# The seam between two transformer-like blocks: token sums as ones-matrix products, a 512-wide norm factor, and another order of the work around it

## What is computed

```
x = rms_norm(x + merged @ w_out, final_g)              # end of the first block
h = concatenate([meta, x])
hn = rms_norm(h, norm1_g)                              # start of the second
f_in, qkv, z, ab, gate_f, gate_d = split(hn @ w_in)
g = -exp(a_log) * softplus(a + dt_bias)                # a, b: 32 columns of ab
beta = sigmoid(b)
qkv = silu(conv5(qkv)); q, k = l2_normalize(q), l2_normalize(k)
... fourier mixing of f_in, gated delta rule forward and backward over q, k, v, g, beta ...
h = h + mixer(h); h = h + mixture_of_experts(h)        # 64 experts, fp32 weights
out = rms_norm(h, final_norm_g)[:, 16:]
```

## Time and profile before

| | |
|---|---|
| median of 3 runs | 1282.62 us (1280.85 to 1285.04) |
| the profiled execution | 1281.57 us, span 1279.6 us |
| instructions | 20485 |
| busy share PE / PEld / DVE / ACT / POOL | 87 / 70 / 37 / 29 / 30 % |
| chain that ended last | PE 59 %, DMA 24 %, DVE 10 %, issue 3 %, ACT 2 % |

### The profile page before, as it was taken

One profiled execution on the slowest core, in us unless ns is written; L12 is line 12 of the kernel. 1 busy time (PEld: TensorE's weight loads), 2 busy tenths in 40 slices (PEclk: granted clock), 3 DMA queues, 4 the chain that ended last, 5 costly groups with the idle time before them and its releaser, 6 DMA issues.

```text
span 1279.6 us, 20485 instructions
## 1 busy us (share of the span) xinstructions
PE 1118.5 (87%) x8376; PEld 893.3 (70%) x8376; DVE 475.8 (37%) x941; ACT 368.5 (29%) x553; POOL 380.7 (30%) x175
## 2 busy tenths in 40 slices
PE   9998999999999799979999999897777776666776
PEld 7987899999999787979888978653333343333334
DVE  3333842911123365543886342321112222211113
ACT  4533334443446364442435200310000000000001
POOL 4834849788776253443103000000000000000000
PEclk8998899999998699989999999998888888888898
DMA  6632636465656233331322037999999999999994
GB/s 227 197 94 71 192 100 181 150 183 181 195 166 192 82 98 100 99 100 34 132 74 98 30 128 305 426 368 427 428 428 430 427 428 428 428 428 427 429 421 182
DMA packets 41554, 304.37 MB, mean 238 GB/s; under 512 B 4869, under 2 KB 5253, under 8 KB 27274
## 3 DMA queue, kind: packets, MB, share of 16 engines
q1 hardware_dynamic: 41194, 302.82, 62.3%
q10 hardware_dynamic: 288, 0.52, 0.1%
HBM read 302.28 MB, written 1.05 MB: 237 GB/s over the span
## 4 chain that ended last, share of the span: by engine, by line
PE 59%; DMA 24%; DVE 10%; issue 3%; ACT 2%; SPq 1%; POOL 1%; DVEq 0%; ACTq 0%
DMA arena<-down 11%; PE bank L426 11%; PE bank L427 11%; PE bank L428 11%; DMA weights<-gate_up 7%; PE bank L759 6%; DMA arena<-gate_up 6%; PE bank L1202 4%; PE bank L1219 4%; DVE arena L2131 2%; DVE arena L2293 1%; DVE arena L2291 1%; POOL rounded L2651 1%; PE bank L701 1%; PE bank L564 1%
## 5 line engine op out<-in xcount | busy, mean ns | idle before, releaser
L2651 POOL TENSOR_TENSOR rounded<-weights,rounded 128x1024 fp32r<-128x1024 f32 x152 | 366.2, 2436 | 244.8 <-ACT rounded L1298 232.5
L426 PE MATMUL bank<-rounded 128*128 128x256 f32 (+2 forms) x784 | 225.8, 288 | 10.1 <-POOL rounded L2651 6.5
L428 PE MATMUL bank<-rounded 128*128 128x256 f32 (+2 forms) x784 | 224.5, 286 | 0.0
L427 PE MATMUL bank<-rounded 128*128 128x256 f32 (+2 forms) x784 | 224.2, 286 | 0.0
L1298 ACT ACTIVATE rounded<-weights 128x1024 fp32r<-128x1024 f32 x146 | 146.8, 1051 | 113.0 <-PE bank L428 91.3
L426 PEld LDWEIGHTS bank<-rounded 128*128 128x128 f32 (+1 forms) x784 | 150.6, 192 | 13.5 <-POOL rounded L2651 7.2
L426 PE MATMUL bank<-rounded,rounded 128*128 128x256 f32 (+3 forms) x472 | 141.3, 301 | 14.2 <-issue 7.5
L427 PEld LDWEIGHTS bank<-rounded 128*128 128x128 f32 (+1 forms) x784 | 150.3, 192 | 0.3 <-issue 0.2
L428 PEld LDWEIGHTS bank<-rounded 128*128 128x128 f32 (+1 forms) x784 | 149.7, 191 | 0.3
L427 PE MATMUL bank<-rounded,rounded 128*128 128x256 f32 (+3 forms) x472 | 139.0, 296 | 0.0
L428 PE MATMUL bank<-rounded,rounded 128*128 128x256 f32 (+3 forms) x472 | 138.9, 296 | 0.0
(11 more groups left out here) (437 smaller groups left out, 1388.2 us busy)
## 6 DMA issues: line engine op xcount, KB each, us to landing
weights<-front SPq DMA_DIRECT2D x152, 512.0 KB, 4.2
arena<-down SPq DMA_DIRECT2D x30, 2048.0 KB, 20.6
weights<-gate_up SPq DMA_DIRECT2D x28, 2048.0 KB, 33.4
arena<-gate_up SPq DMA_DIRECT2D x28, 2048.0 KB, 33.2
weights<-front SPq DMA_DIRECT2D x8, 2048.0 KB, 8.1
arena<-gate_up SPq DMA_DIRECT2D x8, 1024.0 KB, 25.2
weights<-gate_up SPq DMA_DIRECT2D x4, 1024.0 KB, 15.4
arena<-down SPq DMA_DIRECT2D x4, 1024.0 KB, 11.8
```

The lines of the kernel that those rows point to most:

```text
L426: nc.tensor.matmul(out, a[0], b[1], start=start, stop=False)
L427: nc.tensor.matmul(out, a[0], b[0], start=False, stop=False)
L428: return nc.tensor.matmul(out, a[1], b[0], start=False, stop=stop)
L2651: nc.gpsimd.tensor_tensor(lo, raw[q % RAW], hi.bitcast(f32), ALU.subtract).then_inc(sem("w_lo"), 1)
```

## The change

Between the blocks, five edits:

1. TensorE's "sums" uses the 128 x 128 ones matrix as weights and the 256 tokens as the moving side: 4 products instead of 8, and the sums come out on every partition, along the row, 512 wide in bank 7. The two `token_rows` and the wait for "rstd" ahead of them go. `turn[WK] += 2` keeps the rotation of the later banks (and makes it needful to rename the function `turn` to `turn_over`).
2. The factor is therefore worked out on 128 x 512 instead of 128 x 4: three VectorE steps, the root on ScalarE, the reciprocal on VectorE, with `sum_x` as the place for it (`factors2`).
3. The a/b weights' low part (line 2101 of before) moves ahead of fin2, fin3 and the residual on VectorE, so "normed" is 25 before them; on ScalarE the conversions owed for "fin2" and "fin3" move behind the a/b weights' high part.
4. The residual is last, and frees bank 7.
5. ScalarE's chain: the two Abs, then the two Exp, then the two Ln; and the conversions ahead of the chain are those owed for "k2" instead of "ab".

```diff
-        both_g, factors2 = stat(KD), stat(2 * TT)
+        both_g, factors2 = stat(KD), sum_x
...
             fourier_in(0)
-            f = begin("sums")
+            f = begin("sums", (7,))
             for s, src in enumerate((sum_g, sum_x)):
                 pe.wait_ge(sem("sq_pairs"), 12 + s)
-                for t in range(TT):
-                    for i in range(2):
-                        last = nc.tensor.matmul(f.bank[:, 2 * s + t:2 * s + t + 1], src[:, i * SEQ + t * P:i * SEQ + (t + 1) * P],
-                                                ones[:, 0:1], start=i == 0, stop=i == 1)
+                for i in range(2):
+                    last = nc.tensor.matmul(f.bank[:, s * SEQ:(s + 1) * SEQ], ones, src[:, i * SEQ:(i + 1) * SEQ],
+                                            start=i == 0, stop=i == 1)
             end(f, last)
+            turn[WK] += 2
             fourier_in(1)
-            pe.wait_ge(sem("rstd"), 2)
-            token_rows(begin("rows12"), factors2[:, 0:TT])
-            token_rows(begin("rows1", (7,)), factors2[:, TT:])
             fourier_in(2)
...
             act.wait_ge(sem("variance"), 5)
-            nc.scalar.activation(f.bank[:, 8:8 + 2 * TT], factors2, ACT.Sqrt).then_inc(sem("deviation"), 1)
+            nc.scalar.activation(f.bank[:, :], factors2, ACT.Sqrt).then_inc(sem("deviation"), 1)
...
-            lead_for("fin2")
             for j in range(4):
                 act.wait_ge(sem("h_rows"), 4 + j + 1)
                 nc.scalar.activation(hn_hi_r[:, 2 * j:2 * j + 2, META:], two(banks[HN_BANKS[j % 2]]), ACT.Copy).then_inc(sem("h_hi"), 1)
-            lead_for("fin3")
             act.wait_ge(sem("second_in"), 16 * 5)
             nc.scalar.activation(w_ab_hi_r, w_ab, ACT.Copy).then_inc(sem("h_hi"), 1)
+            lead_for("fin2")
...
-            lead_for("ab")
+            lead_for("k2")
             act.wait_ge(sem("ab"), 1)
             for p, t in regions:
-                link(nc.scalar.activation(gx[p, t], gl[p, t], ACT.Abs))
-                link(nc.scalar.activation(gx[p, t], gx[p, t], ACT.Exp, scale=-1.0))
-                link(nc.scalar.activation(gx[p, t], gx[p, t], ACT.Ln, bias=1.0))
+                last = nc.scalar.activation(gx[p, t], gl[p, t], ACT.Abs)
+            link(last)
+            for p, t in regions:
+                last = nc.scalar.activation(gx[p, t], gx[p, t], ACT.Exp, scale=-1.0)
+            link(last)
+            for p, t in regions:
+                last = nc.scalar.activation(gx[p, t], gx[p, t], ACT.Ln, bias=1.0)
+            link(last)
...
-            of_g, of_x = sums.bank[:, 0:TT], sums.bank[:, TT:2 * TT]
-            nc.vector.tensor_scalar(factors2[:, TT:], of_x, 1.0 / D, EPS, ALU.mult, ALU.add)
-            link(nc.vector.tensor_scalar(factors2[:, 0:TT], of_x, EPS / D, EPS * EPS, ALU.mult, ALU.add))
-            nc.vector.scalar_tensor_tensor(factors2[:, 0:TT], of_g, 1.0 / D, factors2[:, 0:TT], ALU.mult,
-                                           ALU.add).then_inc(sem("variance"), 1)
+            of_g, of_x = sums.bank[:, 0:SEQ], sums.bank[:, SEQ:2 * SEQ]
+            link(nc.vector.tensor_scalar(factors2[:, 0:SEQ], of_x, EPS / D, EPS * EPS, ALU.mult, ALU.add))
+            link(nc.vector.scalar_tensor_tensor(factors2[:, 0:SEQ], of_g, 1.0 / D, factors2[:, 0:SEQ], ALU.mult, ALU.add))
+            nc.vector.tensor_scalar(factors2[:, SEQ:], of_x, 1.0 / D, EPS, ALU.mult, ALU.add).then_inc(sem("variance"), 1)
             dve.wait_ge(sem("deviation"), 5)
-            link(nc.vector.reciprocal(factors2, sums.bank[:, 8:8 + 2 * TT]))
+            link(nc.vector.reciprocal(sums.bank[:, :], sums.bank[:, :]))
             dve.sem_inc(sem("rstd"), 1)
-            dve.sem_inc(free[sums.b], 1)
-            rows12 = got("rows12")
+            row12, row1 = sums.bank[:, 0:SEQ], sums.bank[:, SEQ:2 * SEQ]
...
             hn_low(3)
-            take_fourier(2)
-            take_fourier(3)
-            dve.sem_inc(free[rows12.b], 1)
-            f = got("rows1")
-            for k in range(KD):
-                last = nc.vector.scalar_tensor_tensor(res[:, k, META:], res[:, k, META:], col("final_g", k), f.bank[:, 0:SEQ],
-                                                      ALU.mult, ALU.mult)
-            link(last)
-            dve.sem_inc(free[f.b], 1)
             dve.wait_ge(sem("h_hi"), 17)
             link(nc.vector.tensor_tensor(w_ab_lo_r, w_ab, w_ab_hi_r.bitcast(f32), ALU.subtract))
             dve.sem_inc(sem("normed"), 1)
+            take_fourier(2)
+            take_fourier(3)
+            for k in range(KD):
+                last = nc.vector.scalar_tensor_tensor(res[:, k, META:], res[:, k, META:], col("final_g", k), row1,
+                                                      ALU.mult, ALU.mult)
+            link(last)
+            dve.sem_inc(free[sums.b], 1)
```

More of the change, by code:

```diff
@@ L1175, in gather, with turn_over @@
                         last.then_inc(sem("gathered"), 1)
-            def turn(n):
+            def turn_over(n):
                 pe.wait_ge(sem("hid"), n + 2)
@@ L1236, in step @@
                 gather(n + 1, 4 * n + 2)
-                turn(n)
+                turn_over(n)
                 first_products(n + 1, 1 - u)
@@ L1251, in _ @@
                 gather(it + 1, 4 * it + 2)
-                turn(it)
+                turn_over(it)
                 first_products(it + 1, 1, range(KD // 2))
@@ L1256, in _ @@
                 first_products(it + 1, 1, range(KD // 2, KD))
-                turn(it + 1)
+                turn_over(it + 1)
                 def norm_sums(js):
@@ L2060, in hn_rows @@
                     last = nc.vector.scalar_tensor_tensor(banks[HN_BANKS[j % 2]][:, i * SEQ:(i + 1) * SEQ], res[:, k, META:],
-                                                          both_g[:, k:k + 1], rows12.bank[:, 0:SEQ], ALU.mult, ALU.mult)
+                                                          both_g[:, k:k + 1], row12, ALU.mult, ALU.mult)
                 last.then_inc(sem("h_rows"), 1)
@@ L2081, in _ @@
             hn_rows(1)
-            link(nc.vector.tensor_copy(rms2[:, 0:SEQ], rows12.bank[:, 0:SEQ]))
+            link(nc.vector.tensor_copy(rms2[:, 0:SEQ], row12))
             take_fourier(0)
```

## The result

The changed kernel takes 1288.08 us (median of 10 runs, 1284.46 to 1290.60) against 1282.61 (10 runs, 1280.65 to 1285.84) for the kernel before on the same chip: ratio 1.0043, 95% interval 1.0030 to 1.0057. It is slower by 5.5 us, where 2.9 were forecast. The profiled execution took 1290.60 us, span 1288.7; it is the slowest of the ten, 2.5 us above their median.

A forecast was written before the change was run, and what follows sets the result against it. TensorE was taken to set the end up to about 776 us. Chain's end +0.6 and clock loss +2.3 gave +2.9 on 1281.57, 1284.5; with the median 1.05 above, 1285.5 us, range 1279 to 1289.5.

The forecast's parts named there:

- The sums and the norm factor: Start of the seam between the blocks: normed input at 415.9 against 416.61, gain 0.7 us, between 0.9 and -1.4.
- The a/b products: TensorE at the seam: start 5.6 us earlier, 10.4 us near the low clock, K0 6.0 us earlier at 435.4.
- Rival A: Clock holds at 1.00 through a/b products and K0; chain ends 6.7 us earlier: -4.4, 1278.2 us; chance 0.13.
- The two small gaps: TensorE idle about 3 us ahead of fin3 and about 3 us behind it, replacing the 7.54 us gap.
- The conversions moved behind the a/b weights: Weight half 59 converted later; K0's second half wanted only 5 us after K0's start, GpSimd idle: hidden.
- The softplus chain: ScalarE waits until k1 is full, converts 2.0 us, chain 5.2 us: ends at 451.1 against 450.50, 0.6 us later.
- Rival C: Half 61's wait is absent and the chain follows a/b: k3 starts at 446.8, -7.5, 1275.1 us; chance 0.05.
- The new stall: TensorE stands 8.2 us ahead of k3 instead of 1.38; 2.3 us lost to low clock behind it (1.5 to 3.4).
- The sum for the seam: Chain's end +0.6 us plus clock loss behind the stall 2.3 us: +2.9 us.
- the step that came first in the prediction: TensorE sets the end up to about 776 us; a microsecond at the seam is one of the end, no slack.
- the thing that would refute it: Sign: the forecast is wrong if, among others, the stretch from 465 to 776 us changes its length.
- Rival B: Clock returns late at k3 (+1.1), a/b wholly at 0.50 (+0.4), sums at low clock (+0.8): +5.2, 1287.8 us; chance 0.27.

The follow-up runs named there:

- a_lead_ab: Changed kernel with ScalarE's conversions ahead of the softplus chain again those owed for "ab" instead of "k2": 1278.35 us, ratio 0.9970.
- b_lead_k2: Kernel before with only the conversions ahead of the softplus chain changed to those owed for "k2": 1293.26 us, ratio 1.0083.
- b_pad5: Kernel before with five idle products, 2.2 us of TensorE work, put ahead of the first fourier product: 1285.16 us, ratio 1.0025.
- kernels of 8360: The changed kernel, a_lead_ab, b_sums and a_ab_stat, with 8360 TensorE instructions against 8376 in the kernel before; medians 1288.08, 1278.35, 1285.56 and 1278.36 us.
- a_ab_stat: a_lead_ab with the given-up small statistics tile still reserved, so all tiles keep their former addresses: 1278.36 us, ratio 0.9966.
- b_order_grouped: Kernel before with a/b weights early, residual last and the Abs, Exp, Ln chain grouped; narrow sums and "ab" conversions kept: 1274.57 us, ratio 0.9928.
- b_order: Kernel before with a/b weights early and residual last alone, without the grouped chain: 1280.63 us, ratio 0.9987.
- b_grouped: Kernel before with the grouped Abs, Exp, Ln chain alone: 1280.39 us, ratio 0.9986.
- a_pe8: Changed kernel with eight unread one-column products (16 TensorE instructions) added in fin2 and fin3: 1283.37 us, ratio 1.0009.
- b_sums: Kernel before with the ones-matrix sums and the 512-wide factor alone; old order, chain and conversions: 1285.56 us, ratio 1.0025.
- b_sums_pe8: b_sums with eight unread one-column products (16 TensorE instructions) added: 1282.44 us, ratio 0.9998.
- a_ab_pe8: a_lead_ab with eight unread one-column products (16 TensorE instructions) added, four each in fin2 and fin3: 1274.21 us, ratio 0.9931.
- b_pe8: Kernel before with eight unread one-column products (16 TensorE instructions) added: 1283.95 us, ratio 1.0009.

## Why the prediction was right or wrong

**The sums and the norm factor.** Sums full at 409.9 forecast, VectorE starts on them at 409.87. The reciprocal was put at 3.3 us from the slope of 6.2 ns a column and took 3.37 for 512 columns, 6.6 ns. Normed input at 415.9 forecast, 415.39 measured: VectorE's three steps took 1.33 us from the first's start to the last's end, where 1.7 were put.
**The a/b products.** Start 425.0 forecast, 424.40 measured; 10.4 us of them, 10.3 measured, at a clock of 0.56; K0 at 435.4 forecast, 434.7 measured. Rival A (the clock holds) is out. The two small gaps took 3.8 us together instead of about 6. The conversions moved behind the a/b weights were hidden, as forecast: ScalarE is done with them at 427.0 and GpSimd at 433.5, ahead of K0 at 434.7. GpSimd's row, beside the earlier trace rows:

```profile
424.20 9.32 POOL L2648 TENSOR_TENSOR rounded<-weights,rounded 128x1024 fp32r<-128x1024 f32 x4 [11.31 <-ACT rounded L1295]
```

**The softplus chain.** This was the step that decided the seam, and it held. ScalarE's wait until k1 is full: 443.7 forecast, 443.06 measured. (The forecast put 22 instructions into K0's first 5.0 us; the earlier trace rows count 24 there, 22 in a like stretch. With 24 k1 would be full 8.0 us behind K0's start and not 8.3; it was 8.4.) Conversion 2.0, chain 5.2 against 5.1. VectorE released at 451.1 forecast, 450.19 measured, against 450.50 before. Both runs on the argument (a_lead_ab, b_lead_k2) show that the argument, with the wait and the stall that follow from it, costs 10.8 us of the seam in the changed kernel and 11.3 in the one before. Rival C is out. The Trainium skill, "ScalarE: Activation LUTs", What ACT_TABLE_LOAD costs, would have added a drain of 1.38 us to each load; the load starts at 445.31, 0.01 us behind the two Abs (444.98 + 0.32 = 445.30), and the first Exp 0.02 us behind the load's end (445.31 + 1.28 = 446.59, Exp at 446.61), so the trace shows no drain on either side.

**The new stall.** 8.2 us forecast, 7.99 measured; 2.3 us lost to the clock behind it forecast. From k3 to the copy of the sums it is 12.86 us after and 10.27 before: 2.6. The sum for the seam was +2.9; measured +2.3 at the copy, +2.4 from the sums' start.

**What failed** is the step that came first in the prediction: that a microsecond at the seam is a microsecond of the end and nothing else changes up to 776 us. The first half is right (b_lead_k2, b_pad5: +11.3 and +2.2 in, +10.4 and +2.3 out). The second is wrong: the later stretch grew by 4.6 us, twice the seam's own loss, and that is where the time went beyond the forecast. The prediction named this as the thing that would refute it, and gave it no price. The result lies in the stated range, 1279 to 1289.5, but that range was stretched upward for rival B; that it covered a lengthening of the later stretch, which nothing in it priced, is luck. Rival B's number, 1287.8, was the nearest to the result, but for reasons that did not occur: its +2.3 were to come at the seam, behind k3 and in the sums, whose clock was in fact 1.00 after the change.

**What is shown of the cause and what stays open.** Shown by three pairs: 16 instructions in fin2 and fin3 that do nothing useful make a kernel with the wide sums faster by 3 to 5 us in the median (4.7, 3.1, 4.1), and its later stretch shorter by 3.8, 3.2 and 2.4. Shown by the profiles, one execution a kernel: in all four kernels of 8360 TensorE is busy 4.4 to 5.7 us longer in the later stretch than before, at the low clock, in places of the delta rule and just ahead of the release; of waits it has at most 0.9 us more (a_ab_stat). Shown not to be it: tile addresses (a_ab_stat), when the seam ends (b_lead_k2 late by 11.3, b_order_grouped early by 7.3, both near 311 to 312.5), the order (b_order, 311.1). The grouping is at most a small part: b_grouped and b_order_grouped have 312.5, 1.3 to 1.4 us more than the same kernels without it. Not shown is how fewer instructions ahead bring the clock down later. A hint: the program's code comes in by transfers during the run (the page's instruction queues), and one of them comes about 243 us behind the copy of the gate sums in the changed kernel and 231 in a_pe8 (242 and 231 in b_sums and b_sums_pe8, 237 and 232 in a_lead_ab and a_ab_pe8), more apart than the kernels themselves are by then. In the four kernels of 8360 it comes 237 to 243 us behind the copy, in the ten others 230 to 233. Together with the unnamed waits it would fit that TensorE runs out of code at other points. But which engine's code that transfer holds the profile does not say, and the eight products were never put behind the later stretch, which would tell the program's length from the place of its instructions. Nor is it shown that the instructions act by their number: they also fill idle time ahead of the a/b products, and no kernel has them elsewhere. So the code's position is argued, not shown.

## What to carry to other kernels

Before letting an engine do owed work ahead of a wait, look at what the last piece of that work itself waits for: here one weight half more made the softplus chain wait for two projections further on, 11 us for an argument. Take a bundled change apart: order and grouping together gained 7.9 us, the wide sums alone lost 2.7, and the argument lost 10. And where a change takes instructions from a program that is bound by TensorE, compare the length and mean clock of the stretches it doesn't touch; a few microseconds of difference may lie there.

## What the runs showed of the hardware that was not expected

- Eight small products more (16 instructions) made three kernels faster by 3.1 to 4.7 us, with fewer or shorter falls of the granted clock up to some 330 us later. A fourth, with the narrow sums, did not get faster (b_pe8).
- The a/b products ran at 0.56 although the gaps ahead of them were only 2.28 and 1.52 us. Behind the sums the clock was 1.00 after the change; but the narrow sums, at 2.70 us in the earlier trace rows, took between 1.97 and 2.85 us in other executions, so that this is not shown to come of the wide ones.
- A table load follows each change between Exp and Ln in this program, 1.28 us each, with the function starting 0.01 to 0.02 us behind it.
- A 512-wide reciprocal from a PSUM bank took 3.37 us, four times as long a column as a 256-wide step of two operands (0.42).
